# An encoder's opening: squares paired before the angles' sum, modulation blocks on the sync queue, first weight unit in halves

## Chip, cores and metric

One core of a Trainium2 chip runs the whole kernel. The metric is the device time of one execution in microseconds (us). Of the kernel before, three runs were timed: median 1187.73 us, from 1187.71 to 1187.98.

## What is computed

A two-layer encoder trunk on x of 512 tokens by 1024 features, all float32. Cut to what the opening of the kernel touches (layer 0):

```python
c_act = silu(c)                                   # c: (1, 1024)
mod = c_act @ w_ada[l] + b_ada[l]                 # 6 * 1024 values: shift, scale, gate, twice
sh1, sc1, g1, sh2, sc2, g2 = split(mod, 6)
h = rms_norm(x, norm1_g[l]) * (1 + sc1) + sh1
z = h @ w_in[l]                                   # conformer, short conv, q, k, v
cos, sin = rope_tables(positions)                 # angles, used by q and k
```

Behind it stand a gated convolution of 31 taps, a short gated convolution of 3 taps, differential attention of 4 heads, the output projection, and a SwiGLU block with its own modulated norm; the same again for layer 1.

## The kernel before

The kernel is written engine by engine: each engine has one instruction stream in a fixed order, and they meet at semaphores. x lies transposed in SBUF as eight chunks of 128 features by 512 tokens. The weights come as "units" of 128 x 1024 values (512 KB each). The sync queue loads them into two raw slots (`raw`). ScalarE copies a unit with rounding into `w_hi` (`split_hi`), VectorE subtracts it from the raw unit into `w_lo` (`split_lo`), and TensorE takes each product as three matmuls: w_hi with h_hi, w_lo with h_hi, w_hi with h_lo. `w_hi` and `w_lo` are rings of four units. A raw slot is refilled when the unit's `w_lo` is made (semaphore `s_wlo`).

In layer 0 the input projection starts with an a part (conformer, `a_chunk`, 12 matmuls) and a k part (`k_chunk`, 12 matmuls) for each chunk n of h in turn, so that it can run while the chunks are made. The a part of chunks 0 and 1 reads the first and the second 512 columns of unit 0, the k part unit 1; chunks 2 and 3 read units 2 and 3, and so on.

What comes ahead of the first product, by engine:

- TensorE: a few matmuls on ones, two that spread c over the partitions, a warm-up of N_WARM = 14 matmuls of 128 columns on ones, four matmuls that sum the paired squares over the partitions (`s_nstat`), a second warm-up of N_WARM - 3 = 11.
- ScalarE: silu of c, eight squares of x (`s_sq`), a table load, `split_hi(0)`, then Ln and Exp for rstd (`norm_rstd`), and `first_gain(0)`: shift and gain of chunk 0 from the dot products 0 and 1.
- VectorE: `angle_turns`, `sum_angles` (two elementwise steps and a reduce over the terms of each angle), four `pair_squares`, a small step for the gain (`n1b`), `mod_dot(0)` and `mod_dot(1)`, `split_lo(0)`.
- Sync queue: c, positions, frequencies, x in four parts, the small columns (`pcol`), unit 0, then, once modulation block 0 has landed, unit 1.
- GpSimd queue: modulation blocks 0 and 1 once the second part of x has landed, blocks 2 and 3 behind the landing of 0 and 1, each further block when the dot product four before it is done. A block of `w_ada` is 128 x 1024 values, and VectorE makes one shift or scale chunk of it in one instruction (`mod_dot`, accumulating over the row).

Then, for k = 0 to 7, VectorE runs: `norm_apply` (x times gain times rstd, into work_b), `mod_dot(2k+2)`, `norm_lo` (h_lo), `mod_dot(2k+3)`, `split_lo(k+1)`; for k = 0 both dot products stand behind `norm_lo`, with `split_lo(1)` between them; for k = 1 `reduce_angles` (five small steps) stands at the end. ScalarE runs for each k: `norm_hi` (h_hi), `split_hi`, `first_gain(k+1)`. The sines of the angles come on ScalarE at k = 4.

Of the kernel before, what the change touches and what calls it, by code (L numbers as in the profile page):

```python
# [16 lines left out]
T = 512  # L17
# [165 lines left out]
def encoder_kernel(nc, x_in, c_in, pos_in, freq_in, pcol_in, rows_in, ada_in, w_in, out):  # L183
    ctx = ExitStack()
    with ctx:
# [151 lines left out]
        s_raw = [sem(f"raw_landed{i}") for i in range(RAW)]  # L337
        s_whi = sem("weight_hi")
# [13 lines left out]
        s_ada = [sem(f"ada_landed{i}") for i in range(8)]  # L352
        s_ada_gu = [sem(f"ada_gu_landed{i}") for i in range(4)]
# [106 lines left out]
        def ada_landed(eng, m):  # L460

            if M_GU <= m < M_DOWN:
                eng.wait_ge(s_ada_gu[m % 4], 16 * ((m - M_GU) // 4 + 1))
            else:
                before = m // 8 if m < M_GU else M_GU // 8 + (m - M_DOWN) // 8
                eng.wait_ge(s_ada[m % 8 if m < M_GU else (m - M_DOWN) % 8], 16 * (before + 1))
# [13 lines left out]
        def _(sp):  # L480
# [6 lines left out]
            for j in range(RAW):  # L487
                if j == 1:
                    ada_landed(sp, 0)
                sp.dma_start(raw[:, j, :], w_in[j]).then_inc(s_raw[j], 16)  # L490
# [30 lines left out]
        def _(pool):  # L521
# [55 lines left out]
            pool.wait_ge(s_x[KC // 2 - 3], 16)  # L577
            for m in range(2):
                ada_load(m)
# [57 lines left out]
        def _(act):  # L637
# [219 lines left out]
            split_hi(0)  # L857
            norm_rstd(0)
            act.wait_ge(s_pc, 16)
# [3 lines left out]
            for l in range(L):  # L863
                U = UNITS * l
                if l == 0:
                    for k in range(KC):
                        norm_hi(0, 0, k)
                        if k < RING - 1:
                            split_hi(k + 1)
                        else:  # L870
                            step(k - RING + 1)
# [163 lines left out]
        def _(dve):  # L1035
# [37 lines left out]
            def sum_angles():  # L1073

                done(dve.tensor_scalar(whole[:], turns[:], ROUND, None, ALU.add))
                done(dve.scalar_tensor_tensor(turns[:], whole[:], ROUND, turns[:], ALU.subtract, ALU.subtract))
                done(dve.tensor_reduce(ang[:, 0], turns[:], AX_X, ALU.add))
# [329 lines left out]
            sum_angles()  # L1407
# [5 lines left out]
            dve.wait_ge(s_cact, 1)  # L1413
            mod_dot(0)
            mod_dot(1)
            split_lo(0)
            dve.wait_ge(s_nrs, 1)

            for l in range(L):
                U = UNITS * l  # L1420
                if l == 0:
                    for k in range(KC):
# [5 lines left out]
                        if k == 0:  # L1428
                            mod_dot(2)
# [5 lines left out]
                        if k == 1:  # L1435
                            reduce_angles()
# [251 lines left out]
        def _(pe):  # L1688
# [48 lines left out]
            def a_chunk(l, u, n):  # L1737

                r = n % 2
                weights_split(u)  # L1740
# [91 lines left out]
            warm_up(N_WARM)  # L1832
# [4 lines left out]
            warm_up(N_WARM - 3)  # L1837
# [300 lines left out]
```

## Time and profile before

| what | value |
|---|---|
| median of three runs | 1187.73 us |
| span of the profiled execution | 1186.5 us |
| TensorE busy | 1175.3 us, 99% |
| VectorE busy | 728.5 us, 61% |
| ScalarE busy | 506.8 us, 43% |
| GpSimd busy | 119.3 us, 10% |
| HBM traffic over the span | 147 GB/s |

The span runs from the first to the last instruction of one profiled execution; the timed runs are a little longer. Times in the rows count from the span's start. A matmul on float32 data shows as one or more MATMUL records; their ends are modelled, and so the distance from one start to the next tells more than the duration. An elementwise record overlaps with the next of its engine by some 0.07 to 0.1 us, the pipeline's tail. Idle time before a row stands in brackets, with the instruction or the DMA that ended it.

### The profile page before, as it was taken

To read this page: it belongs to the slowest core of one execution; us is meant where nothing else is said; L and a number is where in the kernel's file an instruction comes from. 1 tells how busy PE (TensorE), PEld (TensorE's weight loads), DVE (VectorE), ACT (ScalarE), POOL (GpSimd) and SP (SyncE) were. 2 spreads that over 40 slices of the span, in tenths; PEclk is the share of its full clock that TensorE was granted. 3 is DMA by queue.
4 is the path that set the end of the run, shared out by engine and by line. 5 is a ranking of instruction groups with operands and counts; after the bars stand their busy time and mean duration, and the time that the engine had idled before them with its cause. 6 is when DMAs were issued, how large, how long until landed. Compare 5 with 4: busy or idle time off the path is not lost.

```text
span 1186.5 us, 14451 instructions
## 1 busy us (share of the span) xinstructions
PE 1175.3 (99%) x5168; PEld 929.8 (78%) x5168; DVE 728.5 (61%) x1056; ACT 506.8 (43%) x768; POOL 119.3 (10%) x195
## 2 busy tenths in 40 slices
PE   9999999999999999999999999999999999999998
PEld 6787556878888888888888876678888888888887
DVE  7989998985556432577478998757733333332221
ACT  5546788463222232322234468866523232332220
POOL 2321232211012000121000112100000000000000
PEclk9999999999999999999999999999999999999999
DMA  8777346986565323697323764423332323223332
GB/s 302 249 240 178 80 96 197 307 264 212 186 199 170 106 89 106 227 314 256 106 89 102 165 142 94 85 54 107 107 106 88 106 89 98 96 93 105 105 104 88
DMA packets 48940, 175.18 MB, mean 148 GB/s; under 512 B 5697, under 2 KB 5825, under 8 KB 48898
## 3 DMA queue, kind: packets, MB, share of 16 engines
q1 hardware_dynamic: 30386, 107.13, 27.7%
q0 software_dynamic: 18512, 67.51, 20.4%
q8 instruction: 23, 0.38, 0.1%
q14 instruction: 19, 0.16, 0.0%
HBM read 172.52 MB, written 2.10 MB: 147 GB/s over the span
## 4 chain that ended last, share of the span: by engine, by line
PE 84%; DVE 10%; ACT 4%; issue 2%; DVEq 0%; ACTq 0%; POOL 0%; POOLq 0%
PE ps L1699 22%; PE ps L1700 22%; PE ps L1701 22%; PE ps L1728 3%; DVE uc L1229 3%; PE ps L1765 2%; PE ps L1767 2%; PE ps L1766 2%; PE ps L1732 2%; ACT prob L783 1%; PE ps L1970 1%; DVE neg_max L1333 1%; PE ps L1747 1%; PE ps L1755 1%; PE ps L1748 1%
## 5 line engine op out<-in xcount | busy, mean ns | idle before, releaser
L644 ACT ACTIVATE w_hi<-raw 128x1024 fp32r<-128x1024 f32 x196 | 207.5, 1060 | 519.7 <-PE ps L1701 465.7
L1041 DVE TENSOR_TENSOR w_lo<-raw,w_hi 128x1024 fp32r<-128x1024 f32 x164 | 201.5, 1228 | 240.6 <-ACT w_hi L644 238.5
L1699 PE MATMUL ps<-h_hi,w_hi 128*128 128x512 f32 x832 | 329.0, 395 | 0.0
L1701 PE MATMUL ps<-h_lo,w_hi 128*128 128x512 f32 x832 | 324.1, 390 | 0.0
L1700 PE MATMUL ps<-h_hi,w_lo 128*128 128x512 f32 x832 | 324.1, 389 | 0.0
L1699 PEld LDWEIGHTS ps<-h_hi,w_hi 128*128 128x128 f32 x832 | 156.2, 188 | 48.5 <-issue 17.3
L1701 PEld LDWEIGHTS ps<-h_lo,w_hi 128*128 128x128 f32 x832 | 156.2, 188 | 32.8
L1700 PEld LDWEIGHTS ps<-h_hi,w_lo 128*128 128x128 f32 x832 | 156.3, 188 | 31.2 <-issue 0.5
L1699 PE MATMUL ps<-gu_hi,w_hi 128*128 128x512 f32 x352 | 136.9, 389 | 0.0
L1700 PE MATMUL ps<-gu_hi,w_lo 128*128 128x512 f32 x352 | 136.9, 389 | 0.0
L1701 PE MATMUL ps<-gu_lo,w_hi 128*128 128x512 f32 x352 | 136.9, 389 | 0.0
L1606 DVE TENSOR_TENSOR work_b<-ps,work_a 128x512 f32<-128x512 f32 x42 | 29.0, 692 | 110.0 <-PE ps L1701 86.6
L1229 DVE SCALAR_TENSOR_TENSOR uc<-ua,pcol,uc 128x512 f32<-128x512 f32 x120 | 83.7, 744 | 0.0
L1701 PEld LDWEIGHTS ps<-gu_lo,w_hi 128*128 128x128 f32 x352 | 66.1, 188 | 13.8
L1699 PEld LDWEIGHTS ps<-gu_hi,w_hi 128*128 128x128 f32 x352 | 66.1, 188 | 13.7
L1700 PEld LDWEIGHTS ps<-gu_hi,w_lo 128*128 128x128 f32 x352 | 66.1, 188 | 13.6
L1765 PE MATMUL ps<-w_hi,h_hi 128*128 128x512 f32 x192 | 75.1, 391 | 0.3 <-DVE w_lo L1041 0.3
L1766 PE MATMUL ps<-w_lo,h_hi 128*128 128x512 f32 x192 | 74.7, 389 | 0.0
L1767 PE MATMUL ps<-w_hi,h_lo 128*128 128x512 f32 x192 | 74.7, 389 | 0.0
L783 ACT ACTIVATE prob<-ps,neg_max 128x512 f32<-128x512 f32 x64 | 43.4, 685 | 14.2 <-DVE neg_max L1333 14.0
L1394 DVE SCALAR_TENSOR_TENSOR xT<-ps,mod,xT 128x512 f32<-128x512 f32 x31 | 23.2, 749 | 40.6 <-PE ps L1701 38.4
L530 POOL DMA_DIRECT2D w_lo<-w_stream x32 | 28.1, 879 | 170.6 <-ACT w_lo L639 170.6
(225 smaller groups left out, 1408.9 us busy)
## 6 DMA issues: line engine op xcount, KB each, us to landing
raw<-w_stream SPq DMA_DIRECT2D x196, 512.0 KB, 3.4
w_lo<-w_stream POOLq DMA_DIRECT2D x32, 512.0 KB, 7.9
ada_ring_gu<-ada POOLq DMA_DIRECT2D x28, 512.0 KB, 4.3
ada_ring_late<-ada POOLq DMA_DIRECT2D x28, 512.0 KB, 5.0
ada_ring_first<-ada POOLq DMA_DIRECT2D x16, 512.0 KB, 5.0
ada_ring_mid_a<-ada POOLq DMA_DIRECT2D x12, 512.0 KB, 5.0
ada_ring_mid_b<-ada POOLq DMA_DIRECT2D x12, 512.0 KB, 4.9
xT<-x_t SPq DMA_DIRECT2D x4, 512.0 KB, 5.6
```

The lines of the kernel that those rows point to most:

```text
L644: act.activation(w_hi[:, u % RING, :], raw[:, u % RAW, :], ACT.Copy).then_inc(s_whi, 1)
L783: act.activation(prob[:, it % PROBS, comp, :], ps[:, 2 * (it % 2) + comp, :], ACT.Exp, bias=neg_max[:, it, comp:comp + 1], accum_out=row_s ...
L1041: dve.tensor_tensor(w_lo[:, u % RING, :], raw[:, u % RAW, :], w_hi[:, u % RING, :].bitcast(F32), ALU.subtract).then_inc(s_wlo, 1)
L1229: dve.scalar_tensor_tensor(uc[:, c, :], ua[:, c, j:j + T], w, uc[:, c, :], ALU.mult, ALU.add).then_inc(s_tap, 1)
L1606: dve.tensor_tensor(wb[:, f, :], ps[:, j, :], wa[:, f, :], ALU.mult).then_inc(s_pr, 1)
L1699: pe.matmul(dst, whi, rhs[0][:, n, :], start=start, stop=False)
L1700: pe.matmul(dst, wlo, rhs[0][:, n, :], start=False, stop=False)
L1701: return pe.matmul(dst, whi, rhs[1][:, n, :], start=False, stop=stop)
L1728: pe.matmul(ps[:, bank, :], wp[:, u % RING, n * P:(n + 1) * P], rhs[0][:, n, :], start=b == 0 and wp is w_hi, stop=False)
L1765: pe.matmul(ps[:, bank, :], hs[0], ws[0], start=n == 0, stop=False)
L1766: pe.matmul(ps[:, bank, :], hs[0], ws[1], start=False, stop=False)
L1767: return pe.matmul(ps[:, bank, :], hs[1], ws[0], start=False, stop=n == KC - 1)
```

## The change

Four things are changed, all ahead of layer 0's main part. On VectorE, `sum_angles` is cut in two: its two elementwise steps (`whole_turns`) stay in front, the reduce moves behind `split_lo(2)` at k = 1. `mod_dot(1)` comes before `mod_dot(0)`. Unit 0 is loaded, rounded and subtracted in two halves of 512 columns: the first halves ahead of the loop, the second ones behind `norm_hi` and `norm_lo` of chunk 0; the first half of `w_hi` stands behind `norm_rstd` in place of the whole one ahead of it. Modulation blocks 0 and 1 are issued by the sync queue once the first part of x has landed, ahead of unit 0. The warm-ups go from 14 and 11 matmuls to 9 and 18. The diff:

```diff
--- before.py
+++ after.py
@@ -335,6 +335,9 @@
             return (wa, wb)[t // 2][:, t % 2, :]
 
         s_raw = [sem(f"raw_landed{i}") for i in range(RAW)]
+        s_rawpart = sem("first_half_unit_landed")
+        s_whipart = sem("first_half_unit_hi")
+        s_wlopart = sem("first_half_unit_lo")
         s_whi = sem("weight_hi")
         s_wlo = sem("weight_lo")
         s_nhi = sem("weight_negative_hi")
@@ -350,6 +353,7 @@
         s_const = sem("constants_set")
 
         s_ada = [sem(f"ada_landed{i}") for i in range(8)]
+        s_adafirst = [sem(f"ada_first_landed{i}") for i in range(2)]
         s_ada_gu = [sem(f"ada_gu_landed{i}") for i in range(4)]
         s_cps = sem("c_spread")
         s_cact = sem("c_act_ready")
@@ -461,9 +465,12 @@
 
             if M_GU <= m < M_DOWN:
                 eng.wait_ge(s_ada_gu[m % 4], 16 * ((m - M_GU) // 4 + 1))
+            elif m < 2:
+                eng.wait_ge(s_adafirst[m], 16)
             else:
                 before = m // 8 if m < M_GU else M_GU // 8 + (m - M_DOWN) // 8
-                eng.wait_ge(s_ada[m % 8 if m < M_GU else (m - M_DOWN) % 8], 16 * (before + 1))
+                slot = m % 8 if m < M_GU else (m - M_DOWN) % 8
+                eng.wait_ge(s_ada[slot], 16 * (before + (slot >= 2)))
 
         def chunks_before(k):
 
@@ -484,10 +491,13 @@
             for i in range(KC // 2):
                 sp.dma_start(xT[:, 2 * i:2 * i + 2, :], x_in[:, 2 * i:2 * i + 2, :]).then_inc(s_x[i], 16)
             sp.dma_start(pcol[:], pcol_in).then_inc(s_pc, 16)
-            for j in range(RAW):
-                if j == 1:
-                    ada_landed(sp, 0)
-                sp.dma_start(raw[:, j, :], w_in[j]).then_inc(s_raw[j], 16)
+            sp.wait_ge(s_x[0], 16)
+            for m in (1, 0):
+                sp.dma_start(ada_slot(m), ada_in[m]).then_inc(s_adafirst[m], 16)
+            sp.dma_start(raw[:, 0, 0:T], w_in[0][:, 0:T]).then_inc(s_rawpart, 16)
+            sp.dma_start(raw[:, 0, T:UE], w_in[0][:, T:UE]).then_inc(s_raw[0], 16)
+            ada_landed(sp, 0)
+            sp.dma_start(raw[:, 1, :], w_in[1]).then_inc(s_raw[1], 16)
             begin = RAW
             for l in range(L):
 
@@ -574,9 +584,6 @@
             pool.affine_select(out=ident[:], in_=ident[:], compare_op=ALU.not_equal, fill=1.0, base=0,
                                pattern=[[-1, P]], channel_multiplier=1).then_inc(s_const, 1)
             pads()
-            pool.wait_ge(s_x[KC // 2 - 3], 16)
-            for m in range(2):
-                ada_load(m)
             for m in range(2, 4):
                 ada_landed(pool, m - 2)
                 ada_load(m)
@@ -854,8 +861,9 @@
                 act.activation(sq0[:, k, :], xT[:, k, :], ACT.Square).then_inc(s_sq, 1)
             act.preload_act_table_set("natural_log_exp_and_others")
             act.wait_ge(s_const, 2)
-            split_hi(0)
             norm_rstd(0)
+            act.wait_ge(s_rawpart, 16)
+            act.activation(w_hi[:, 0, 0:T], raw[:, 0, 0:T], ACT.Copy).then_inc(s_whipart, 1)
             act.wait_ge(s_pc, 16)
             act.wait_ge(s_n1b, 1)
             first_gain(0)
@@ -865,6 +873,9 @@
                 if l == 0:
                     for k in range(KC):
                         norm_hi(0, 0, k)
+                        if k == 0:
+                            unit_raw_wait(act, 0, 0, 0)
+                            act.activation(w_hi[:, 0, T:UE], raw[:, 0, T:UE], ACT.Copy).then_inc(s_whi, 1)
                         if k < RING - 1:
                             split_hi(k + 1)
                         else:
@@ -1070,10 +1081,13 @@
                 dve.wait_ge(s_sq, 2 * i + 2)
                 dve.tensor_tensor(sq0[:, 2 * i, :], sq0[:, 2 * i, :], sq0[:, 2 * i + 1, :], ALU.add).then_inc(s_pair, 1)
 
-            def sum_angles():
+            def whole_turns():
 
                 done(dve.tensor_scalar(whole[:], turns[:], ROUND, None, ALU.add))
                 done(dve.scalar_tensor_tensor(turns[:], whole[:], ROUND, turns[:], ALU.subtract, ALU.subtract))
+
+            def sum_angles():
+
                 done(dve.tensor_reduce(ang[:, 0], turns[:], AX_X, ALU.add))
 
             def reduce_angles():
@@ -1404,16 +1418,18 @@
                                              ALU.mult, ALU.add).then_inc(done, 1)
 
             angle_turns()
-            sum_angles()
+            whole_turns()
             for i in range(KC // 2):
                 pair_squares(i)
             dve.wait_ge(s_pc, 16)
             dve.scalar_tensor_tensor(n1b[:], pcol[:, 0, C_BADA + 1:C_BADA + 2 * KC:2], 1.0, pcol[:, 0, C_N1:C_N1 + KC],
                                      ALU.add, ALU.mult).then_inc(s_n1b, 1)
             dve.wait_ge(s_cact, 1)
+            mod_dot(1)
             mod_dot(0)
-            mod_dot(1)
-            split_lo(0)
+            dve.wait_ge(s_whipart, 1)
+            dve.tensor_tensor(w_lo[:, 0, 0:T], raw[:, 0, 0:T], w_hi[:, 0, 0:T].bitcast(F32),
+                              ALU.subtract).then_inc(s_wlopart, 1)
             dve.wait_ge(s_nrs, 1)
 
             for l in range(L):
@@ -1426,6 +1442,9 @@
                             mod_dot(2 * k + 2)
                         norm_lo(0, 0, k)
                         if k == 0:
+                            dve.wait_ge(s_whi, 1)
+                            dve.tensor_tensor(w_lo[:, 0, T:UE], raw[:, 0, T:UE], w_hi[:, 0, T:UE].bitcast(F32),
+                                              ALU.subtract).then_inc(s_wlo, 1)
                             mod_dot(2)
                             split_lo(1)
                         if k + 1 < KC:
@@ -1433,6 +1452,7 @@
                         if k:
                             split_lo(k + 1)
                         if k == 1:
+                            sum_angles()
                             reduce_angles()
                     first = KC - RING + 1
                 else:
@@ -1737,7 +1757,10 @@
             def a_chunk(l, u, n):
 
                 r = n % 2
-                weights_split(u)
+                if u == 0 and n == 0:
+                    pe.wait_ge(s_wlopart, 1)
+                else:
+                    weights_split(u)
                 if l:
                     pe.wait_ge(s_yghi, n + 1)
                 else:
@@ -1829,12 +1852,12 @@
             for b in range(2):
                 mm = pe.matmul(ps[:, b, :], ones[0:1, :], c_row[:, b * T:(b + 1) * T], start=True, stop=True)
             mm.then_inc(s_cps, 1)
-            warm_up(N_WARM)
+            warm_up(N_WARM - 5)
             for k in range(0, KC, 2):
                 pe.wait_ge(s_pair, k // 2 + 1)
                 mm = pe.matmul(ps[:, B_STAT, :], ones[:], sq0[:, k, :], start=k == 0, stop=k == KC - 2)
             mm.then_inc(s_nstat, 1)
-            warm_up(N_WARM - 3)
+            warm_up(N_WARM + 4)
 
             for l in range(L):
                 U = UNITS * l
```

## Rows read from the trace of the kernel before

**Rows 1.** The page's busy time, share of the span and instructions of each engine.

```profile
PE 1175.3 (99%) x5168; PEld 929.8 (78%) x5168; DVE 728.5 (61%) x1056; ACT 506.8 (43%) x768; POOL 119.3 (10%) x195
```

**Rows 2.** Timeline, TensorE, 19 to 36 (start us, us, what, idle before and its releaser).

```profile
19.69 0.47 PE L1747 MATMUL ps<-h_hi,w_hi 128*128 128x512 f32 x1 [1.16 <-ACT h_hi L733]
...
32.24 0.47 PE L1747 MATMUL ps<-h_hi,w_hi 128*128 128x512 f32 x1 [0.47 <-ACT h_hi L733]
...
35.49 0.50 PE L1765 MATMUL ps<-w_hi,h_hi 128*128 128x512 f32 x1 [0.27 <-DVE w_lo L1041]
```

**Rows 3.** Busy time by stretch (us, then busy us of each engine, PEclk, DMA, GB/s).

```profile
38.00:44.00 6.00, 6.00 (x28) 4.96 (x27) 6.00 (x10) 3.69 (x6) 1.12 (x3) 1.00 0.93 336
```

**Rows 4.** TensorE's waits, 36 to the end (us in total, times, longest).

```profile
PE ps L1958 <- DVE prob L1348: 2.1, 5, 0.7
```

**Rows 5.** Timeline, VectorE, 18 to 36.

```profile
18.04 0.75 DVE L1117 SCALAR_TENSOR_TENSOR work_b<-xT,gain,rstd 128x512 f32<-128x512 f32 x1 [0.97 <-ACT gain L723]
...
19.58 0.75 DVE L1125 SCALAR_TENSOR_TENSOR h_lo<-work_b,mod,h_hi 128x512 fp32r<-128x512 f32 x1 [0.79 <-ACT h_hi L733]
...
24.40 0.75 DVE L1117 SCALAR_TENSOR_TENSOR work_b<-xT,gain,rstd 128x512 f32<-128x512 f32 x1 [0.64 <-ACT gain L723]
...
29.16 0.22 DVE L1081 TENSOR_SCALAR ang<-ang 128x128 f32<-128x128 f32 x1
...
30.59 0.75 DVE L1117 SCALAR_TENSOR_TENSOR work_b<-xT,gain,rstd 128x512 f32<-128x512 f32 x1
...
34.21 1.23 DVE L1041 TENSOR_TENSOR w_lo<-raw,w_hi 128x1024 fp32r<-128x1024 f32 x1
```

**Rows 6.** Timeline, VectorE, before 18.

```profile
9.39 1.35 DVE L1077 TENSOR_REDUCE ang<-turns 128x128 f32<-128x1152 f32 x1
...
10.78 2.50 DVE L1071 TENSOR_TENSOR sq_first<-sq_first 128x512 f32<-128x512 f32 x4
...
13.54 1.22 DVE L1094 SCALAR_TENSOR_TENSOR ada_ring_first<-ada_ring_first,c_b 128x1024 f32<-128x1024 f32 x1 [0.18 <-DMA ada_ring_first<-ada]
...
14.70 1.23 DVE L1094 SCALAR_TENSOR_TENSOR ada_ring_first<-ada_ring_first,c_b 128x1024 f32<-128x1024 f32 x1
```

**Rows 7.** Timeline, ScalarE, before 18.

```profile
7.38 4.32 ACT L854 ACTIVATE sq_first<-xT 128x512 f32<-128x512 f32 x8
...
13.01 1.06 ACT L644 ACTIVATE w_hi<-raw 128x1024 fp32r<-128x1024 f32 x1
...
16.11 0.69 ACT L713 ACTIVATE rstd<-ps,eps 128x512 f32<-128x512 f32 x1 [2.04 <-PE ps L1835]
...
16.83 0.63 ACT L715 ACTIVATE rstd<-rstd 128x512 f32<-128x512 f32 x1
...
17.36 0.28 ACT L721 ACTIVATE mod<-mod_raw,pcol 128x1 f32<-128x1 f32 x1
...
17.55 0.37 ACT L723 ACTIVATE gain<-mod_raw,n_biased,pcol 128x1 f32<-128x1 f32 x1
```

**Rows 8.** Timeline, TensorE, before 19.

```profile
6.35 6.29 PE L1706 MATMUL ps<-ones 128*128 128x128 f32 x28
...
12.47 3.60 PE L1835 MATMUL ps<-sq_first,ones 128*128 128x512 f32 x8
...
15.91 2.62 PE L1706 MATMUL ps<-ones 128*128 128x128 f32 x22
```

**Rows 9.** Timeline, GpSimd's DMA issues, before 14.

```profile
7.88 1.29 POOL L525 DMA_DIRECT2D ada_ring_first<-ada  x2 [6.03 <-DMA xT<-x_t]
...
13.73 0.53 POOL L525 DMA_DIRECT2D ada_ring_first<-ada  x1 [4.56 <-DMA ada_ring_first<-ada]
```

**Rows 10.** DMA queues from 10 to 11 (packets, MB, share of 16 engines).

```profile
q1 hardware_dynamic: 144, 0.38, 94.6%
q0 software_dynamic: 8, 0.03, 8.2%
```

**Rows 11.** TensorE's busy time and DMA by stretch of 1 us (last: GB/s).

```profile
12.00:13.00 1.00, 1.00 (x6) 1.00 1.04 426
```

## Prediction

> **What bounds the kernel now.** I read the page first: TensorE (PE) is busy for 99% of the span [rows 1]. A change to the opening can therefore pay only by what it takes out of TensorE's gaps, and 1187.73 us is mostly 1150 us of work that is untouched. So the second view is TensorE's timeline of the opening, for its gaps. The first product of the input projection starts at 19.69, after a gap; another gap stands before 32.24; the last one ends at 35.49, where the k part of chunk 2 waited for VectorE's (DVE's) w_lo of unit 3 [rows 2]. The third view is the busy time by stretch: from 38 to 44 PE is busy for 6.00 of 6.00 us [rows 3], and the list of waits from 36 to the end has only short ones (the largest group is 2.1 us in five waits, all inside attention) [rows 4]. They hang on work that itself follows PE. So what counts is **the moment at which unit 3's w_lo is done, 35.4**: the end moves with that, one for one, and not with the moment at which the first product starts. This is the thing to see.
>
> The fourth view is VectorE's timeline from 18 to 36 [rows 5]. From the first scaled chunk (work_b, 18.04) to the end of unit 3's w_lo it stops only twice for ScalarE (ACT): for h_hi (0.79, until 19.58) and for the next gain (0.64, until 24.40). From 24.40 on, each row starts where the one before ends. So every instruction put on VectorE between 18.04 and 34.21 moves 35.49 by its whole length, and whatever starts the chain earlier pulls it forward by as much.
>
> **What sets 18.04.** Before it lie, in order: VectorE's pair sums, TensorE's four statistics matmuls, ScalarE's Ln and Exp, the two small gain activations, then work_b. The statistics matmuls start at 12.47 [rows 8], when the first warm-up ends, although the first pair (10.78, four of them in 2.50) is ready by 11.46 [rows 6]; Ln follows at 16.11 [rows 7].
>
> **The parts.** (1) Pair sums ahead of the angles' reduce. The reduce takes from 9.39 to 10.78, 1.39 with its wait [rows 6]. Without it, pair 0 starts at 9.39. ScalarE's eight squares run at 0.54 each from 7.38 (4.32 for eight) [rows 7], so squares 1, 3, 5 and 7 are done by about 8.5, 9.6, 10.7 and 11.7. With 0.68 for a sum, the pairs are ready at 10.1, 10.7, 11.4 and 12.4.
>
> (2) Warm-up shorter by 5 matmuls, that is 10 rows in the profile (each has two). The 28 rows before the statistics run from 6.35 to 12.47, 0.219 a row; the 22 behind them are (2.62 - 0.27) / 21 = 0.112 apart [rows 8]. The granted-clock column shows full speed in both, so the spacing has to be read: it is the spacing of 1.2 GHz in the first and of 2.4 GHz in the second. The statistics' eight rows are (3.60 - 0.59) / 7 = 0.43 apart, thus already fast: the clock rose at about 12.4. Now the statistics would start at 12.47 - 2.19 = 10.28, **before that rise**. PE's stream up to there is the same as before and stays full behind it, so I take the rise at the same 12.4. At the slow level a row takes 0.43 x 0.219 / 0.112 = 0.84. Rows one and two then last until 11.96; the third is half done at 12.4 and ends at 12.6; five more at 0.43 give 14.76, and with the tail of 0.16 the sum is there at 14.92, Ln at 14.96: 1.15 earlier than 16.11. (All eight rows fast, bounded by pair 3 at 12.4, would give Ln at about 13.5, 2.6 earlier.)
>
> The page "TensorE: Matmul & The Clock Gate" of the Trainium skill, Part 1, has the rule that the moment of the rise is not tied to the kernel's start and differs from run to run. This trace is one execution and shows the rise only once, at about 12.4. By the rule the rise may also come before 10.3; that is a rival below.
>
> (3) Unit 0 in halves. Before, its w_hi (1.06) ran at 13.01, while ScalarE waited for the statistics anyway: it was free [rows 7]. Now the first half stands between Exp and the gain. A 512-column activation takes 0.54 of ScalarE's time by the squares. So ScalarE goes: Ln 14.96, Exp 15.68, half w_hi 16.21, mod 16.75, gain 16.94 to 17.31, and work_b at 17.43; of VectorE's side, half w_lo starts at 16.85 and takes 0.60 to 0.68 (a pair sum has the same size), so 17.47. **The chain starts at 17.47 in place of 18.04: -0.57.** The other half of w_lo comes behind the first h_lo, inside VectorE's chain: **+0.60**. The other half of w_hi lies in ScalarE's slack behind h_hi (0.54, when VectorE is busy with h_lo), and the whole w_hi of unit 1 and the wait for the next gain come later than both; zero. If that cover were gone it would cost at most its 0.54.
>
> (4) The angles' reduce now stands behind unit 2's w_lo, just ahead of reduce_angles at 29.16. That is in the stretch without a gap [rows 5], and so it costs what it cost at 9.39: **+1.39** with its own wait. Behind it in VectorE's queue are work_b of chunk 2, two dot products, h_lo and unit 3's w_lo, for which PE waits. The sines at 44 on ScalarE need the result much later; zero.
>
> (5) DMAs. Sync waits for the first part of x, then issues blocks 1 and 0, then the two halves of unit 0, all while the queue still has 3 us of x to move. GpSimd (POOL) loses two issues. In the trace the transfers go in order of issue: with q0's blocks issued from 7.88 on [rows 9], q1 still moved 0.38 MB and q0 only 0.03 MB between 10 and 11 [rows 10]. At the 0.43 MB per us of such a stretch [rows 11] the total before 14 is unchanged; the two blocks now stand ahead of unit 0 (0.52 MB, 1.25 us). Block 1 should land at about 12.1, block 0 at 13.5 as before (its dot started at 13.54, ended by that DMA [rows 6]), the first half of unit 0 at 14.0, the second at 14.6. VectorE's dots run from 12.6 to 13.8 and to 15.0 (1.16 each, from 13.54 to 14.70 [rows 6]), all before 16.75; the halves are needed at 16.21 and about 18.9. Block 2 is issued at 13.73 [rows 9] as before and is needed at 20.3. The wait on sync delays unit 0 by nothing that is needed. Value zero; below zero is excluded, since nothing on the chain waits for these loads. Upper bound: if the landings came later by as much as one 512 KB block (1.25 us), block 0 would still be in time by the dot product's margin of 1.7; if by two, 2.5 - 1.7 = 0.8.
>
> The second warm-up, 18 matmuls, is 36 x 0.112 = 4.0 from 14.76, so 18.8; the first product may start at 17.47 + 1.65 (19.69 less 18.04) = 19.1. Zero.
>
> **The sum**: -0.57 + 0.60 + 1.39 = +1.4 us. Unit 3's w_lo ends at 36.8 in place of 35.4, although the first product starts 0.6 earlier. The profiled span of 1186.5 becomes 1187.9; the median of the runs lies 1.2 above the span, and 1187.73 + 1.4 = **1189.1 us**, 0.12% more. A difference under 0.2% (2.4 us) can't be told from no change here, so this forecast is "same". Ends of the terms: start -0.3 to -0.9, half w_lo 0.57 to 0.68, reduce 1.35 to 1.45: +1.1 to +1.8.
>
> **Rivals.**
> A, the clock is up before the statistics start, so that pair 3 bounds them: Ln at 13.5, work_b at 16.0, start term -2.0, in all 0.0: 1187.7, and up to 1188.3 for a rise in between. For: the sums are ready early enough. Against: in the one trace of it PE's same stream was slow until 12.4. 14%.
> B, what is moved is covered after all: the reduce and the half w_lo fall into a gap that opens in VectorE's stretch, and only the earlier start is left: 1187.73 - 0.57 = 1187.2, at best with A 1185.7. For: VectorE did have 0.64 of idle before 24.40. Against: no row from 24.40 on shows idle time before it. 5%.
> C, **slower than can be overlooked**: the clock does not rise until the statistics are over, since the run-up was cut. Eight rows at 0.84 from 10.28 end at 17.0, with the tail 17.2; work_b at 19.8, +1.7; with 0.60 and 1.39 that is +3.7: 1191.4. It decides from a rise later than about 14.5 on. Against: PE has no idle time between 6.35 and there in either kernel. 4%.
> D, late loads (part 5), by up to 0.8: 1189.5 to 1190.0. 6%.
> The forecast has the other 71%. None gives faster by over 0.2% (1185.4) except the best end of B with A: 1%. Slower by over 0.2% (1190.1): C and the edge of D, 5%. Same: 94%. The range goes from 1187.5 to 1190.2: it takes in the forecast with its ends, most of A and D, and leaves out B, C and A's lowest end.
>
> **What would show it.** In the changed kernel's trace: reduce behind the w_lo of unit 2 with no idle time ahead of it; the statistics' first rows about 0.84 apart and the rest 0.43; work_b first at 17.4; first product at 19.1; PE's last gap of the opening at about 36.9, again ended by w_lo; from there on no new waits. Wrong if that gap ends before 35.5, if a DMA ends a wait of VectorE or ScalarE before 18, or if the sum of PE's waits behind 37 differs by over 0.5 us.

## The result, and the profile after

Over 20 runs each, the changed kernel has a median of 1189.57 us (1189.20 to 1190.45), the kernel before 1187.74 us (1187.41 to 1188.29). The ratio is 1.0016 with a 95% interval of 1.0009 to 1.0022: slower by 1.83 us, 0.15%. The forecast was 1189.1 us in a range of 1187.5 to 1190.2, and "same" within 0.2%.

The page of the changed kernel (profiled span 1188.6 us), its span and its busy times; compare [rows 1]:

```profile
span 1188.6 us, 14462 instructions
PE 1175.4 (99%) x5172; PEld 930.4 (78%) x5172; DVE 728.9 (61%) x1057; ACT 507.1 (43%) x769; POOL 117.7 (10%) x193
```

TensorE's busy time is the same to 0.1 us, and the time is lost in its gaps. (That the sums agree so closely is an accident: the two warm-ups together take 0.9 us less, and one stretch described below takes 1.1 more.) The timeline of TensorE in the changed kernel (start us, us, what; in brackets the idle time before and what ended it):

```profile
10.05 2.41 PE L1858 MATMUL ps<-sq_first,ones 128*128 128x512 f32 x5
...
18.01 0.47 PE L1770 MATMUL ps<-h_hi,w_hi 128*128 128x512 f32 x1 [0.24 <-ACT h_hi L740]
...
22.36 0.50 PE L1788 MATMUL ps<-w_hi,h_hi 128*128 128x512 f32 x1 [1.38 <-DVE w_lo L1052]
...
33.33 0.54 PE L1770 MATMUL ps<-h_hi,w_hi 128*128 128x512 f32 x1 [1.89 <-ACT h_hi L740]
33.66 0.63 PE L1771 MATMUL ps<-h_hi,w_lo 128*128 128x512 f32 x1
...
37.75 0.39 PE L1788 MATMUL ps<-w_hi,h_hi 128*128 128x512 f32 x1
```

Against [rows 2], the first product starts 1.7 us earlier (18.01 for 19.69), the a part of chunk 2 starts 1.1 us later (33.33 for 32.24) behind a gap of 1.89, and the k part of chunk 2 starts 2.26 us later (37.75 for 35.49). From there to the end of the span it is 1150.9 us in this profile and 1151.0 in the one before. So the whole difference between these two profiles is made ahead of 38. The profile shown is of the slowest of the 20 runs (1190.45 us); a second one, of a typical run, comes in the next section.

VectorE's timeline in the same profile has the three places to see: the wait for a DMA at the dot product of block 2, the reduce between unit 2's w_lo and chunk 2's work_b, and the halves; compare [rows 5, 6]:

```profile
9.31 2.02 DVE L1082 TENSOR_TENSOR sq_first<-sq_first 128x512 f32<-128x512 f32 x3
...
16.37 0.75 DVE L1131 SCALAR_TENSOR_TENSOR work_b<-xT,gain,rstd 128x512 f32<-128x512 f32 x1
...
18.57 0.69 DVE L1446 TENSOR_TENSOR w_lo<-raw,w_hi 128x512 fp32r<-128x512 f32 x1
...
19.94 1.23 DVE L1108 SCALAR_TENSOR_TENSOR ada_ring_first<-ada_ring_first,c_b 128x1024 f32<-128x1024 f32 x1 [0.68 <-DMA ada_ring_first<-ada]
...
24.09 0.75 DVE L1131 SCALAR_TENSOR_TENSOR work_b<-xT,gain,rstd 128x512 f32<-128x512 f32 x1 [0.64 <-ACT gain L730]
...
28.85 1.35 DVE L1091 TENSOR_REDUCE ang<-turns 128x128 f32<-128x1152 f32 x1
...
31.67 0.75 DVE L1131 SCALAR_TENSOR_TENSOR work_b<-xT,gain,rstd 128x512 f32<-128x512 f32 x1
...
35.30 1.22 DVE L1052 TENSOR_TENSOR w_lo<-raw,w_hi 128x1024 fp32r<-128x1024 f32 x1
```

From chunk 1's work_b to chunk 2's it took 6.19 us before and takes 7.58 now: +1.39. The last thing is in the busy time by stretch of the changed kernel (stretch, its length in us; then the busy us of TensorE, its weight loads, VectorE, ScalarE, GpSimd; granted clock, DMA share, GB/s):

```profile
33.60:36.90 3.30, 3.30 (x9) 2.55 (x8) 3.30 (x5) 1.10 (x3) 1.05 (x2) 0.50 0.46 164
37.70:44.00 6.30, 6.30 (x29) 5.18 (x29) 6.30 (x11) 4.71 (x7) 1.58 (x3) 1.00 0.88 295
```

Behind the 1.89 us gap the granted clock is 0.50 (1.2 GHz) for the a part of chunk 2, whose matmuls follow each other at 0.43 us instead of 0.23. Unit 3's w_lo is done at 36.52 here, and TensorE starts the k part only at 37.75: in this execution TensorE itself is the later one. That was in none of the forecast's cases. It is not in every execution, as the next section shows.

### The profile page after: what moved, and what is told of

Same layout as the page of the kernel before. It is cut to its first block, busy times and chain, and to the rows that moved or that the text cites. A ratio compares the mean times of both kernels' runs of the same rounds, so it can differ in the third digit from the quotient of the medians.

```text
span 1188.6 us, 14462 instructions
## 1 busy us (share of the span) xinstructions
PE 1175.4 (99%) x5172; PEld 930.4 (78%) x5172; DVE 728.9 (61%) x1057; ACT 507.1 (43%) x769; POOL 117.7 (10%) x193
## 4 chain that ended last, share of the span: by engine, by line
PE 79%; DVE 13%; ACT 4%; DMA 2%; issue 2%; SPq 0%; DVEq 0%; ACTq 0%
PE ps L1719 21%; PE ps L1721 21%; PE ps L1720 21%; DVE uc L1243 3%; PE ps L1748 3%; PE ps L1790 2%; PE ps L1788 2%; PE ps L1789 2%; ACT prob L790 1%; PE ps L1752 1%; DVE neg_max L1347 1%; PE ps L1993 1%; PE ps L1770 1%; PE ps L1771 1%; DMA ada_ring_first<-ada 1%
```

## The experiments

Each kernel ran beside the kernel before on the same chip; the medians there were 1187.69 (e1 to e4), 1187.63 (e6, e7) and 1187.55 (e8 to e11). Line numbers in rows are those of each kernel's own file. A table of marks comes first, read from each kernel's profile: "Ln" is ScalarE's Ln for rstd, wb0 to wb2 are VectorE's work_b of chunks 0 to 2, "dot 2" the dot product of block 2, "k2" TensorE's first matmul of the k part of chunk 2. The median is of all runs of a kernel, the marks are of one execution.

| kernel | median us | Ln | wb0 | dot 2 | wb1 | wb2 | k2 |
|---|---|---|---|---|---|---|---|
| before, first profile | 1187.74 | 16.11 | 18.04 | 20.25 | 24.40 | 30.59 | 35.49 |
| before, second (b_again) | 1187.37, one time | 15.20 | 17.13 | 19.34 | 23.49 | 29.68 | 34.58 |
| changed, first profile | 1189.57 | 13.86 | 16.37 | 19.94 | 24.09 | 31.67 | 37.75 |
| changed, second (a_again) | 1189.45, one time | 14.67 | 17.18 | 19.99 | 24.14 | 31.71 | 36.61 |
| e1, reduce moved alone | 1189.24 | 15.53 | 17.46 | 19.66 | 23.82 | 31.40 | 36.30 |
| e3, changed, reduce in front | 1189.06 | 15.24 | 17.76 | 20.56 | 24.71 | 30.90 | 35.80 |
| e4, changed, filler | 1189.36 | 13.90 | 16.42 | 19.62 | 23.78 | 31.36 | 36.26 |
| e6, before, steps behind unit 3 | 1186.54 | 15.18 | 17.21 | 19.41 | 23.56 | 28.32 | 33.49 |
| e7, changed, block 3 later | 1189.96 | 14.10 | 16.61 | 19.42 | 23.57 | 31.15 | 36.05 |
| e8, changed, reduce in the wait | 1188.13 | 14.37 | 16.95 | 19.76 | 23.91 | 30.09 | 34.99 |
| e9, e8 and steps behind unit 3 | 1188.08 | 14.43 | 17.01 | 19.82 | 23.96 | 28.72 | 33.90 |
| e10, changed, warm-up of 14 | 1191.42 | 15.89 | 18.40 | 21.21 | 25.36 | 32.93 | 38.85 |
| e11, changed, unit 0 whole | 1190.14 | 14.96 | 18.43 | 20.63 | 24.78 | 32.35 | 37.24 |

### The reduce alone, in the kernel before

```diff
-            sum_angles()
+            whole_turns()
...
                         if k == 1:
+                            sum_angles()
                             reduce_angles()
```

> The kernel before, with one change: the reduce of the angles moves from the front to behind unit 2's w_lo (k = 1). Theory T (VectorE's unbroken stretch sets when unit 3's w_lo is done, and with it the end): the statistics still start where the first warm-up of 14 ends, the reduce costs its 1.39 us, work_b of chunk 2 comes at about 32.0 instead of 30.59, and the median is 1187.7 + 1.4 = 1189.1 us; the gap of TensorE before the a part of chunk 2 grows from 0.5 to 1.9 us. Theory F (beside T, a second cost: TensorE's clock falls to 1.2 GHz in or behind that longer gap): up to 1.3 us more, 1190.4, with rows of the a part of chunk 2 spaced 0.43 instead of 0.23. Rival N (the move is free, the loss of the whole change lies in its opening): 1187.7.

Measured: 1189.24 us (1188.77 to 1190.14), ratio 1.0015 (1.0006 to 1.0024). From wb1 to wb2 it is 7.58 against 6.19. Moving this one instruction by itself costs 1.55 us, the greater part of the 1.83. TensorE and VectorE in this kernel's timeline:

```profile
33.05 0.47 PE L1751 MATMUL ps<-h_hi,w_hi 128*128 128x512 f32 x1 [1.86 <-ACT h_hi L733]
36.30 0.50 PE L1769 MATMUL ps<-w_hi,h_hi 128*128 128x512 f32 x1 [0.24 <-DVE w_lo L1041]
```

```profile
28.58 1.35 DVE L1080 TENSOR_REDUCE ang<-turns 128x128 f32<-128x1152 f32 x1
```

Rival N (the move is free) falls. Theory F fits in part: in 5 of the 11 runs the mean granted clock is below 1.000, and those have a median of 1189.76 against 1189.17 for the other six; the profile shown is one of the six, so where the clock fell in the five isn't seen.

### The reduce elsewhere

At k = 3, with the five small steps at k = 4 and the sines at k = 5:

```diff
-                        if k == 1:
+                        if k == 3:
                             sum_angles()
+                        if k == 4:
                             reduce_angles()
...
-                        if k == 4:
+                        if k == 5:
                             act.wait_ge(s_ang, N_ANGLE)
```

> The changed kernel, with the angles' reduce at k = 3, its five small steps at k = 4 and the sines at k = 5, where VectorE is ahead of TensorE. Theory T: 1.39 + 1.43 us leave the stretch that ends with unit 3's w_lo; that is done at about 33.6, TensorE is then the later one and starts the k part of chunk 2 at about 34.0 without a gap, 1.5 us before the 35.49 of the kernel before: 1186.2 us (1186.0 to 1186.7). Theory F: no gap over 1 us stands before chunk 2, so no fall of the clock either. Rival N (the loss is in the opening): stays at 1189.5. Rival L (VectorE gets late again at chunks 4 to 6): 1187 to 1188, with waits of TensorE for h_hi there.

Measured: 1192.37 us (1189.65 to 1193.60, 5 runs), 4.7 us slower than before and a clear miss. The first half of the theory held: wb1 to wb2 fell to 4.77 (24.64 to 29.41). But in its profile block 2 landed late (a wait of VectorE of 1.10), TensorE stood still for 1.79 us ahead of 22.91, and the clock was at 0.50 from 24 to 27. So k2 came at 35.52, with TensorE the later one. The chunks behind it paid for the rest: from k2 to the end it is 1155.0 us, where most other profiles have about 1151. TensorE's wait, the busy time by stretch, and ScalarE's wait for the raw unit of unit 8's w_hi:

```profile
22.91 0.50 PE L1789 MATMUL ps<-w_hi,h_hi 128*128 128x512 f32 x1 [1.79 <-DVE w_lo L1052]
```

```profile
24.00:27.00 3.00, 3.00 (x8) 2.32 (x7) 2.36 (x5) 2.14 (x4) 0.69 (x2) 0.50 0.98 363
```

```profile
68.41 1.06 ACT L651 ACTIVATE w_hi<-raw 128x1024 fp32r<-128x1024 f32 x1 [3.04 <-DMA raw<-w_stream]
```

In b_again the first w_hi behind the sigmoids starts without a DMA wait at 64.51. A raw slot is refilled when VectorE has made a w_lo; the angle work at k = 3 and 4 made those later, and the refills met GpSimd's four modulation blocks issued from 60.02 on. That account fits the rows but was not tried by itself. In four of the five runs the mean granted clock is below 1.000, so that part of the 4.7 may be the clock's. Rival L names nearly the right place and too small a price.

Back in front of the pair sums, the rest as changed:

```diff
             whole_turns()
+            sum_angles()
             for i in range(KC // 2):
...
-                            sum_angles()
                             reduce_angles()
```

> The changed kernel, with the reduce back in front of the pair sums. Theory T: pairs ready at 11.4 to 13.3 as before, so Ln at about 14.3 with the clock up, 0.5 later than in the changed kernel's profile (13.86), work_b at 16.8; then the half w_lo (0.6) and the wait for block 2 stay, the 1.39 goes. Unit 3's w_lo is done at about 34.8 to 35.0 instead of 35.4 before: median 1187.0 to 1187.3, and no gap over 1.5 us before chunk 2, so no fall of the clock. Rival N (the opening costs, not the moved reduce): 1189 or more.

Measured: 1189.06 us (1188.66 to 1191.56), ratio 1.0018 (1.0008 to 1.0027). The 1.39 is gone between wb1 and wb2 (6.19 again), and no run has a mean clock below 1.000. But the start came later than expected: the statistics start at 11.44, where the first pair sum is ready, and take four times 0.86, so Ln is at 15.24 and not at 14.3; my expectation counted from the last pair, not from TensorE's own 3.5 us:

```profile
11.44 3.70 PE L1858 MATMUL ps<-sq_first,ones 128*128 128x512 f32 x8 [1.08 <-DVE sq_first L1082]
```

So wb0 is at 17.76, 0.6 behind b_again's 17.13, and 6.95 instead of 6.36 lie between wb0 and wb1 (the half w_lo). 0.63 + 0.59 = 1.22 later at k2 (35.80 for 34.58), for 1.37 measured. **The changed opening, without the moved reduce, is a loss of its own.** The expectation (1187.0 to 1187.3) failed, and its rival, that the opening costs, holds. Four of the eleven runs lie at 1190.46 to 1191.56 at full clock; why is open.

The start's 0.63 has, but for 0.04, one cause. Ln comes when it came in b_again (15.24 and 15.20), but from Ln to wb0 it takes 2.52 instead of 1.93, because the half w_hi now stands between Exp and the gain. So the halves cost 0.59 ahead of wb0 and 0.59 behind it. In the kernel before, unit 0's w_hi ran in ScalarE's wait for the statistics [rows 7]. Now the two modulation blocks stand ahead of unit 0 on the queue: its first half is issued at 7.20 and landed 6.9 later, at 14.1, behind the changed kernel's Ln at 13.86 (in e3, with Ln at 15.24, it would have been in time); before, the whole unit was issued at 4.54 and landed 7.6 later, at 12.1. No run has the halves with the loads in their old order, so how the 1.2 divides between the two changes is not shown.

The start also explains why the parts don't add up: e1's 1.55 and e3's 1.37 are together more than the whole's 1.83. With the short warm-up, taking the reduce away from the front brings Ln forward (15.24 in e3, 14.67 and 13.86 in the changed kernel); in e1, where the warm-up is the long one, it brings nothing in the one profile taken (15.53, against 15.20 in b_again). From e3 to a_again k2 moves by -0.57 and +1.38, together 0.81 (35.80 to 36.61); with the 1.22 above that is the 2.03 between b_again and a_again.

In the wait that the changed order leaves on VectorE:

```diff
             mod_dot(0)
+            sum_angles()
             dve.wait_ge(s_whipart, 1)
```

> The changed kernel, with the reduce of the angles moved once more: on VectorE between the two dot products and the half w_lo of unit 0, where VectorE waits for ScalarE (about 1.0 us from 14.77, up to 1.8 where the clock rises late). Theory T: of the 1.39 us nothing to 0.4 is left; from work_b of chunk 0 to work_b of chunk 2 it takes 13.1 to 13.2 us instead of 14.5; the k part of chunk 2 starts at 35.2 to 35.5, the median is 1188.1 to 1188.5 (1.2 below the changed kernel's 1189.57), and so still 0.5 to 0.8 above the kernel before: the half w_lo's 0.6. Rival (the loss is mostly elsewhere): above 1189.0.

Measured: 1188.13 us (1187.61 to 1188.63), ratio 1.0004 (0.9995 to 1.0013), as theory T had it; k2, at 34.99, is 0.2 ahead of its range. VectorE's timeline: the reduce at 14.78 and then work_b with nothing lost; wb0 is 2.58 behind Ln, against 2.51 in the changed kernel.

```profile
14.78 1.35 DVE L1091 TENSOR_REDUCE ang<-turns 128x128 f32<-128x1152 f32 x1
16.95 0.74 DVE L1131 SCALAR_TENSOR_TENSOR work_b<-xT,gain,rstd 128x512 f32<-128x512 f32 x1
```

The same instruction costs 1.4 us at 28.85 and about 0.1 at 14.78. That is a matter of place alone.

### The small steps behind unit 3's w_lo

In the kernel before, alone:

```diff
-                        if k == 1:
+                        if k == 2:
                             reduce_angles()
```

> The kernel before, with one change: the five small steps of the angles (reduce_angles, 1.43 us) move from behind unit 2's w_lo (k = 1) to behind unit 3's (k = 2). Theory T (what stands on VectorE ahead of unit 3's w_lo moves the end one for one, until TensorE itself is the later one; what stands behind it has slack): unit 3's w_lo is done 1.43 earlier, the gap of TensorE before the a part of chunk 2 shrinks from 0.5 to 0, the k part of chunk 2 starts 1.1 to 1.2 earlier, with nothing given back at chunk 3, whose scaled x comes when it came before: median 1186.5 (1186.3 to 1186.8). Rival: chunk 3 gives it back, or a later wait does: 1187.7.

Measured: 1186.54 us (1186.08 to 1188.63), 1.09 below the kernel before on that chip; ratio 0.9993, interval 0.9984 to 1.0002. TensorE in this kernel's timeline: the list of its waits between 28 and 38 is empty, and these are the two starts.

```profile
30.77 0.39 PE L1747 MATMUL ps<-h_hi,w_hi 128*128 128x512 f32 x1
...
33.49 0.39 PE L1765 MATMUL ps<-w_hi,h_hi 128*128 128x512 f32 x1
```

k2 starts 1.09 before b_again's 34.58. It is the counterpart of e1: 1.4 us out of VectorE's stretch give 1.1, and there the gain ends, since TensorE is then itself the later one. This is the fastest kernel of the study; the interval of its ratio still includes 1.

On top of e8:

```diff
-                        if k == 1:
+                        if k == 2:
                             reduce_angles()
```

> As the one before, and the five small steps of the angles stand behind unit 3's w_lo (k = 2). Theory T: unit 3's w_lo is done 1.43 earlier again, TensorE itself is the later one from chunk 1 on, without a gap before the a part of chunk 2; its k part starts at 33.9 to 34.2; median 1186.9 to 1187.2, 0.5 to 0.8 below the kernel before, and above the 1186.54 of the kernel before with the steps moved alone, since the half w_lo delays unit 1's w_lo and chunk 1. Rival (the changed opening is worth something once VectorE's stretch is short enough): 1186.3 or less.

Measured: 1188.08 us (1187.22 to 1188.75), no better than e8's 1188.13. In its profile k2 starts at 33.90 as expected, 1.09 before e8's, and its time of 1187.22 is the lowest of the eleven. From the list of TensorE's waits between 110 and 300:

```profile
PE ps L1748 <- DMA w_lo<-w_stream: 1.3, 1, 1.3
```

Part of what is won at 34, 0.5 us in this profile (1151.5 between k2 and the end, 1151.0 in e8), is given back near 245, where a w_lo loaded by DMA is waited for. In b_again's list there are two short waits for h_hi (0.3 each) and not this one. The median missed its expectation by 1.0, and why most runs give back more than this one is open. The opening's changes were not made to pay by this.

### The opening's parts

Warm-ups as before (14 and 11), the rest as changed:

```diff
-            warm_up(N_WARM - 5)
+            warm_up(N_WARM)
...
-            warm_up(N_WARM + 4)
+            warm_up(N_WARM - 3)
```

> The changed kernel, with the warm-ups of the kernel before (14 matmuls ahead of the statistics, 11 behind). Theory T: the statistics start where the first warm-up ends, at 11.2 (clock up by 9.8) to 12.4 (late rise), Ln at 14.9 to 16.1, work_b of chunk 0 2.5 behind Ln: 17.4 to 18.6, block 2 is never waited for; the k part of chunk 2 starts 19.4 behind work_b: 36.8 to 38.0, median 1189.9 to 1190.6, so the shorter warm-up is worth 0.3 to 1.0. Rival (the start is bounded by block 2's landing in most executions): as the changed kernel, 1189.5.

Measured: 1191.42 us (1189.85 to 1191.84, 7 runs). wb0 is at 18.40, 2.51 behind Ln, and from wb0 to wb2 it takes 14.53, the same as in a_again (14.53). So the earlier start by the shorter warm-up is real and worth 1.2 between these two profiles. It is less where the clock rises early: here the statistics start at 12.19, in b_again with the same warm-up at 11.46. The median is 0.8 above the expected range, and the clock is the likely reason: in six of seven runs the mean granted clock is below 1.000; the seventh has 1189.85. The busy time by stretch of one of the six shows the fall:

```profile
35.90:38.90 3.00, 3.00 (x9) 2.33 (x8) 3.00 (x5) 1.00 (x3) 0.53 (x1) 0.50 0.75 217
39.00:45.00 6.00, 6.00 (x28) 4.96 (x27) 6.00 (x11) 4.67 (x7) 1.43 (x3) 0.99 0.94 328
```

Unit 0 in one piece:

```diff
-            sp.dma_start(raw[:, 0, 0:T], w_in[0][:, 0:T]).then_inc(s_rawpart, 16)
-            sp.dma_start(raw[:, 0, T:UE], w_in[0][:, T:UE]).then_inc(s_raw[0], 16)
+            sp.dma_start(raw[:, 0, :], w_in[0]).then_inc(s_raw[0], 16)
...
             norm_rstd(0)
-            act.wait_ge(s_rawpart, 16)
-            act.activation(w_hi[:, 0, 0:T], raw[:, 0, 0:T], ACT.Copy).then_inc(s_whipart, 1)
+            split_hi(0)
```

> The changed kernel with unit 0 in one piece again: one load, its w_hi (1.05) between Exp and the gain, its w_lo (1.14) ahead of chunk 0's work_b. Theory T: work_b of chunk 0 comes 2.5 + 1.0 = 3.5 behind Ln instead of 2.5, from there to chunk 1's work_b it takes 6.36 instead of 6.96 where no DMA is waited for; both together +0.4, median 1189.8 to 1190.1. Rival (the second half of w_lo costs nothing, the halves are a gain of 1.0): 1190.5.

Measured: 1190.14 us (1189.64 to 1190.56), as expected but for 0.04. wb0 is 3.47 behind Ln, and wb0 to wb1 takes 6.35 again. So the half w_lo inside VectorE's stretch costs 0.6, as forecast, and the halves together are still worth 0.3 to 0.6 once unit 0 is loaded behind the modulation blocks (k2 at 37.24 for a_again's 36.61, of which 0.3 is the later Ln; 0.57 between the medians).

### The wait for block 2

> The kernel before, unchanged, for one more profile. Theory P (the moment at which TensorE's clock rises to 2.4 GHz differs from run to run, and the first profile, with the rise at about 12.4, was a late one): the rise comes earlier than 12.4, Ln at 15.1 to 15.9 instead of 16.11, work_b of chunk 0 at 17.0 to 17.9 instead of 18.04, span 1185.6 to 1186.4. Rival: the rise is tied to the kernel's own start, all rows within 0.1 of the first profile.

> The changed kernel, unchanged, for one more profile. Theory P: Ln between 13.8 and 14.95, work_b of chunk 0 between 16.3 and 17.5. Theory Q (block 2 lands about 6 us after its issue, since blocks 3 to 5 are issued right behind it): its dot product starts at 19.6 to 20.4 whatever the start was, ended by that DMA where work_b came before 16.9. A fall of the clock behind the gap before chunk 2 may or may not be there.

Two more executions of the unchanged pair, in this order. In b_again the first warm-up, the statistics and chunk 0's work_b:

```profile
6.36 5.14 PE L1706 MATMUL ps<-ones 128*128 128x128 f32 x28
...
11.46 3.70 PE L1835 MATMUL ps<-sq_first,ones 128*128 128x512 f32 x8
```

```profile
17.13 0.75 DVE L1117 SCALAR_TENSOR_TENSOR work_b<-xT,gain,rstd 128x512 f32<-128x512 f32 x1
```

Against [rows 5, 7, 8], the same 28 rows of the warm-up take 5.14 us instead of 6.29, the statistics start 1.0 earlier and everything from Ln on 0.9, and its time of 1187.37 (span 1185.5) lies at the bottom of the kernel's runs. Theory P holds: the first profile was of a late rise of the clock. With an early rise it is the pair sums that set the start: the first is ready at 11.4, and e3, whose warm-up is the short one, starts its statistics no earlier (11.44). The shortened warm-up has nothing to win there but by the moved reduce. In a_again the eight rows of the statistics take 4.21 instead of 3.70, which fits first ones at the slow level, as the forecast had it, though fewer of them: it had 4.6. Theory Q does not hold in general: here block 2 landed 4.3 us behind its issue, in the first profile of the same kernel 6.2.

```profile
10.35 4.21 PE L1858 MATMUL ps<-sq_first,ones 128*128 128x512 f32 x8
```

```diff
                 ada_landed(pool, m - 2)
+                if m == 3:
+                    pool.wait_ge(s_raw[0], 16)
                 ada_load(m)
```

> The changed kernel, where the GpSimd queue waits for the second half of unit 0 before it issues modulation block 3 (at about 14.9 instead of 14.3), so that blocks 3 to 5 go out about as they did before. Theory Q: block 2 lands 4.4 to 4.9 us behind its issue (18.2 to 18.6) instead of 6.2; no DMA ends a wait of VectorE at its dot product, which starts at 19.25 where Ln is at 13.9; unit 3's w_lo is done 0.7 earlier; median 0.3 to 0.7 below the changed kernel's, 1188.9 to 1189.3. Rival: the landing depends on the total queued and not on the distance of the issues; it stays at 19.6 to 20.4 and the median at 1189.5.

Measured: 1189.96 us (1189.19 to 1191.47); block 2 landed 5.3 us behind its issue and wasn't waited for. Since the same issue takes from 4.3 to 6.2 us in the changed kernel itself, the distance to block 3 doesn't explain it; theory Q falls, and what makes that landing vary is open. The median isn't lower, and the profile shows one more cause of spread, far from the opening. ScalarE waits for a raw unit in layer 0's output projection, and TensorE then for the sum of squares:

```profile
232.63 1.06 ACT L653 ACTIVATE w_hi<-raw 128x1024 fp32r<-128x1024 f32 x1 [2.90 <-DMA raw<-w_stream]
```

```profile
PE ps L1806 <- DVE sq_sum L1404: 1.3, 1, 1.3
```

### The fall of the clock

```diff
+                        if n == 2:
+                            for _ in range(8):
+                                pe.matmul(ps[:, 0, 0:P], ones[:], zeros[:], start=False, stop=False)
                         a_chunk(l, U + A_AT[l][n // 2], n)
```

> The changed kernel, with eight matmuls of ones by a tile of zeros (128 columns, added to a bank in use, so they add nothing) in TensorE's gap before the a part of chunk 2. They take 1.8 us of a gap of 1.9. Theory F (the clock falls in some executions because TensorE stands still there, and this costs up to 1.3 us of them): no rows at the slow level behind 20 us, median 0.2 to 0.6 below the changed kernel's 1189.57, the spread over executions narrower (about 0.5 instead of 1.25 us). Rival G (the fall is due to the earlier gaps at 21 and 25 us, or happens in few executions only): median as the changed kernel's, 1189.5.

Measured: 1189.36 us (1188.75 to 1190.13), 0.2 below the changed kernel's, at the edge of what was expected. The spread, 1.38, isn't narrower, against the expected 0.5; so something other than the fall spreads these runs. The mean granted clock is below 1.000 in 1 run of 11. The median alone doesn't tell theory F from rival G, and neither does 1 of 11 against the changed kernel's own 3 of 20. The comparison over all kernels is stronger. Where TensorE stands still for 1.8 to 1.9 us ahead of chunk 2, it is below 1.000 in 3 of 20 (changed), 5 of 11 (e1), 4 of 11 (e7), 6 of 7 (e10) and 5 of 11 (e11): 23 of 60 runs. Where that gap is about 0.5 or less, in none of 44 (e3, e6, e8, e9) and in 3 of the 77 of the kernel before, one of which, at 0.949, stands apart. e2 has no gap there and yet 4 of 5 runs below 1.000; its profile shows the fall behind its 1.79 us of idle time at 22.91. So a long gap goes with the fall, but the mean over a run doesn't say where it happened: it was seen in place in three profiles (changed, e10, e2). Why the share goes from 3 of 20 to 6 of 7 for nearly the same gap is open. The price in place is 1.14 us: chunk 1's and 2's work_b stand at the same times in the two profiles of the changed kernel, and k2 at 37.75 and 36.61. The medians of runs with and without differ by less, 0.1 (e11), 0.2 (changed), 0.6 (e1) and 0.9 (e7), and by 1.6 in e10, where only one run is without.

## Why the prediction was right, and where its terms were off

**What bounds the end**: right where the clock stays up. In all profiles here but e2's and e7's, 1150.9 to 1151.5 us lie between k2 and the end of the span. The moment of unit 3's w_lo, and not the first product, carries the result. Two things limit it: where the clock falls, TensorE is later than that w_lo (k2 1.2 behind it in the changed kernel's first profile, 1.1 in e10's), and in e2, e7 and some runs of e3 more is lost behind k2.

**The reduce, +1.39**: right within 0.01 (7.58 less 6.19 between wb1 and wb2, in both profiles of the changed kernel and in e1).

**The half w_lo, +0.60**: right (6.96 less 6.36 between wb0 and wb1 in a_again and b_again), and confirmed by e11.

**The start, -0.57**: the term that was mis-sized. It is made of Ln's 1.15 earlier and of 0.58 for the half w_hi in front of the gain. The second part was right (2.51 from Ln to wb0 in the changed kernel, 1.93 before). Of the first, the changed kernel's side was about right: Ln forecast at 14.96, measured 14.67 and 13.86; wb0 forecast at 17.47, measured 17.18 and 16.37. The other side was wrong: I subtracted from 18.04, one execution with a late rise of the clock. b_again's wb0 is at 17.13, where the pair sums set the start. Against it Ln is only 0.53 earlier in a_again, the half w_hi takes 0.58, and the start term is +0.05 (17.18 less 17.13). The sum is then 0.05 + 0.60 + 1.39 = 2.04, and k2 is 36.61 against 34.58, 2.03; the two times differ by 2.08 and the medians of 20 by 1.83. b_again is itself a fast run (1187.37 for a median of 1187.74). By 0.37 for that, a typical wb0 of the kernel before is at about 17.5 and the start term about -0.3, an estimate from these numbers; then the sum is 1.7. The two profiles of each kernel differ by the moment of the clock's rise: statistics at 12.47 and 11.46 before, Ln at 13.86 and 14.67 in the changed kernel. The rule of the Trainium skill's page "TensorE: Matmul & The Clock Gate", Part 1, that the moment of the rise differs from run to run, was weighed against the changed kernel alone. These traces agree with it, and it bears on the kernel before just as much.

**The offset** of 1.2 us between span and time was off for the same reason: the pairs of one execution give 1.7 to 1.9 (1190.45 and 1188.6, 1189.45 and 1187.6, 1187.37 and 1185.5). The 1.2 was a late execution's span subtracted from the median. It drops out of the forecast, which adds the change to the median. Nor was the claim right that a difference under 0.2% can't be told from none: the interval of the ratio, 1.0009 to 1.0022, leaves out 1.

**Rival A** (the clock up early) came true for the changed kernel's first profile: Ln at 13.86 for a forecast 13.5, wb0 at 16.37. It was priced at a whole 0.0 and was worth less, for a reason that the forecast passed over: with work_b at 16.4, block 2 is needed at 19.2, and it landed at 19.9. I had checked its landing against 20.3 only. The 0.68 of waiting took back most of the earlier start: wb1 is at 24.09 and 24.14 in the two profiles, whatever wb0 was.

**Rival B** (covered) falls with e1. **C** (no rise until the statistics are over) was seen in no profile, but it looked at the wrong place: the clock fell behind the gap that the reduce opened in front of chunk 2. The forecast's own numbers would have shown that gap: it put the reduce there and gave no thought to the 1.9 us in which TensorE then stands still. **D** is the wait of 0.68, with another block than the one that I had bounded. Of the signs that were to show the forecast wrong none came: no DMA ended a wait of VectorE or ScalarE before 18. But a new wait is there behind k2 in the first profile, 1.0 for a w_lo loaded by DMA, though the time from k2 to the end is the same.

Between the first profiles the first product comes 1.7 earlier (18.01 for 19.69), and a reader who judged by it would have called the change a gain. Between the second ones it isn't earlier (18.83 for 18.78).

## What to carry to other kernels

Find the last wait of a stage, and count what stands on its releasing engine between the stage's start and that wait; an earlier start is worth nothing if more work is moved into that stretch than is taken off ahead of it. Put work without a deadline into a wait that the trace shows, or behind the last instruction that the bound engine waits for, and look at what waits behind that: the small steps gained 1.1 us in e6 (its interval still includes no gain), while the reduce at k = 3 with the steps at k = 4 lost 4.7 (e2). And before a start is compared with one profile, see from a second whether it is a typical one: here it moved by 0.9 us, more than the term that was being worked out.

## What was not expected of the hardware

TensorE's granted clock fell to 1.2 GHz behind idle time of 1.79 us (e2), 1.85 us (e10) and 1.89 us (changed, where gaps of 1.38 and 0.38 stood in the 12 us before). In the last two it was back at 2.4 GHz when the k part of that chunk began, with TensorE at work in between. The section "HAM oscillation" of the Trainium skill's page "TensorE: Matmul & The Clock Gate" tells of such falls behind clearly longer waits. These traces show them behind shorter ones. In 23 of 60 runs of the kernels with such a gap ahead of chunk 2 the mean clock is below 1.000. The one fall that can be priced in place cost 1.14 us, and it shows in a median only where it is frequent. A 512 KB transfer issued by GpSimd at the same point of the same kernel landed 4.3 us behind its issue in one execution and 6.2 in another.
